# Ending the index stage of an expert-routing step on GpSimd instead of VectorE, in a two-layer decoder kernel on one Trainium2 core

## The reference

```python
    sv, si = lax.top_k(sc, PEER_TOPK)
    cand = sv[:, :, 0, :, None] + sv[:, :, 1, None, :]
    cidx = si[:, :, 0, :, None] * PEER_NKEYS + si[:, :, 1, None, :]
    cs, cpos = lax.top_k(cand.reshape(t, PEER_HEADS, -1), PEER_TOPK)
    idx = jnp.take_along_axis(cidx.reshape(t, PEER_HEADS, -1), cpos, axis=-1)
    gate = jax.nn.softmax(cs, axis=-1)
...
        act = jax.nn.gelu(jnp.einsum('td,tkd->tk', xbb, u_tab[ib], preferred_element_type=jnp.float32))
        return jnp.einsum('tk,tkd->td', gb * act, v_tab[ib].astype(jnp.float32))
```

## Time and profile before

| | |
|---|---|
| median of 3 runs | 1553.53 us (1551.04 to 1553.55) |
| profiled execution, its own time | 1553.37 us |
| its span in the profile | 1551.6 us |
| busy, share of the span | PE 71%, PEld 22%, DVE 72%, ACT 50%, POOL 38% |
| chain that ended last | DMA 32%, DVE 31%, PE 22%, ACT 7% |
| moved by DMA | 603.39 MB, mean 389 GB/s |
| gathers (software queue) | 536.90 MB, 84.8% of the DMA engines' time |

### The profile page before, as it was taken

One profiled execution on the slowest core, in us unless ns is written; L12 is line 12 of the kernel. 1 busy time (PEld: TensorE's weight loads), 2 busy tenths in 40 slices (PEclk: granted clock), 3 DMA queues, 4 the chain that ended last, 5 costly groups with the idle time before them and its releaser, 6 DMA issues.

```text
span 1551.6 us, 19133 instructions
## 1 busy us (share of the span) xinstructions
PE 1097.8 (71%) x5920; PEld 348.4 (22%) x5920; DVE 1111.5 (72%) x2533; ACT 770.2 (50%) x2120; POOL 589.4 (38%) x517
## 2 busy tenths in 40 slices
PE   7997678866765666679866575656878666666665
PEld 3542222322211212223221121212323111111110
DVE  2356887479787899985477799999456866666554
ACT  2315554445456667764334666766334644444433
POOL 0024343323443354554334345344432443434430
PEclk9998689878966776879988567686998777676675
DMA  9569999999999998999999999999999999999995
GB/s 358 179 234 413 420 405 418 414 415 408 415 421 421 354 374 358 410 421 415 412 413 414 403 357 369 355 363 406 380 416 415 415 422 421 421 421 421 421 422 234
DMA packets 105418, 603.39 MB, mean 389 GB/s; under 512 B 9314, under 2 KB 9442, under 8 KB 39780
## 3 DMA queue, kind: packets, MB, share of 16 engines
q0 software_dynamic: 73728, 536.90, 84.8%
q1 hardware_dynamic: 31588, 65.26, 11.3%
HBM read 601.08 MB, written 1.05 MB: 388 GB/s over the span
## 4 chain that ended last, share of the span: by engine, by line
DMA 32%; DVE 31%; PE 22%; ACT 7%; issue 3%; DVEq 3%; ACTq 1%; POOL 1%; SPq 0%; POOLq 0%
DMA rings<-in_uv_tab_dram,idx 24%; DVE rings L1324 11%; PE ps L715 9%; PE ps L920 8%; DMA wst<-in_wq_dram 7%; DVE mem L1231 2%; PE ps L908 2%; DVE dgs L1324 2%; ACT dgs L667 1%; DVE mem L1213 1%; ACT wgt L664 1%; DMA rings<-in_w_in_dram 1%; DVE mem L1242 1%; ACT L661 1%; DVE mem L1240 1%
## 5 line engine op out<-in xcount | busy, mean ns | idle before, releaser
L920 PE MATMUL ps<-rings,dgs 64*64 64x512 f32 x3648 | 638.0, 804 | 343.3 <-ACT dgs L667 342.6
L463 POOL DMA_INDIRECT rings<-in_uv_tab_dram,idx x456 | 521.7, 1144 | 804.3 <-PE ps L920 687.8
L1324 DVE CUSTOM_DVE_ANT_0 rings<-rings,h 128x1024 f32<-128x1024 f32 x456 | 550.7, 1224 | 210.8 <-DMA rings<-in_uv_tab_dram,idx 197.7
L661 ACT ACTIVATE gel<-dots 128x1 f32<-128x1 f32 x512 | 102.1, 199 | 522.2 <-DVE dots L1324 518.5
L920 PEld LDWEIGHTS ps<-rings,dgs 64*64 64x64 f32 x3648 | 128.3, 163 | 783.4 <-ACT dgs L667 682.3
L667 ACT ACTIVATE dgs<-cst,wgt 128x128 f32<-128x128 f32 x512 | 205.6, 402 | 36.3 <-issue 1.5
L715 PE MATMUL ps<-wst,hT 128*128 128x512 f32 x320 | 168.0, 666 | 37.1 <-DMA wst<-in_wq_dram 20.5
L664 ACT ACTIVATE wgt<-gel,share 128x1 f32<-128x1 f32 x512 | 150.8, 295 | 35.5 <-issue 0.3
L920 PE MATMUL ps<-dgs 64*64 64x512 f32 x448 | 80.2, 795 | 53.2 <-ACT dgs L667 53.1
L463 POOL DMA_INDIRECT dgs<-in_uv_tab_dram,idx x56 | 65.9, 1176 | 88.3 <-PE ps L920 74.8
L715 PEld LDWEIGHTS ps<-wst,hT 128*128 128x128 f32 x320 | 63.4, 212 | 138.1 <-issue 134.9
(11 more groups left out here) (192 smaller groups left out, 991.2 us busy)
## 6 DMA issues: line engine op xcount, KB each, us to landing
wst<-in_wq_dram SPq DMA_DIRECT2D x15, 2048.0 KB, 28.2
wst<-in_w_out_dram SPq DMA_DIRECT2D x4, 2048.0 KB, 22.8
wst<-in_glu_w_dram SPq DMA_DIRECT2D x4, 2048.0 KB, 31.7
rings<-in_uv_tab_dram,idx POOLq DMA_INDIRECT x456, 15.7
rings<-in_w_in_dram SPq DMA_DIRECT2D x3, 2048.0 KB, 16.7
rings<-in_w_in_dram SPq DMA_DIRECT2D x2, 1024.0 KB, 7.5
dgs<-in_w_in_dram SPq DMA_DIRECT2D x1, 2048.0 KB, 19.4
vec<-in_vecs_dram SPq DMA_DIRECT2D x3, 512.0 KB, 17.2
```

The source lines that it names most:

```text
L463: nc.gpsimd.indirect_dma_start(out=ring[g % RING], out_offset=None, in_=uv_tab, in_offset=bass.IndirectOffsetOnAxis(ap=idx[n % AHEAD][:, s ...
L661: A.activation(gel[i][:, every], dots[i][:, every], ACT.Gelu_apprx_tanh)
L920: ins = PE.matmul(ps[64 * b:64 * b + 64, 4 + 2 * t + half, :], diag[rows, g % DIAGS, rows], ring[g % RING][rows, D + b * BANK:D + (b + 1) ...
L1324: V.tensor_tensor_reduce(out=u, in0=u, in1=h[:, t, :], scale=1.0, scalar=0.0, op0=ALU.mult, op1=ALU.add, accum_out=dots[n % 2][:, s:s + 1] ...
```

## The change

DVE now does the whole of `route_best` and the first half of the index stage in one go at slot R+4: the four bits and the comparison, into a tile of its own, `hot_p`. The last steps go to POOL: product with the key numbers (512 elements per partition), four additions that each halve the last axis (256, 128, 64 and 32 elements), one addition of the two halves (16) and a copy to the integer tile (16), with a drain behind each. The factor 128 is now put into `top_f` on DVE. POOL runs stages of the table six slots late (`POOL_LAG`): the route whose index stands at R+6 is done right before gather R+12. A new semaphore, `pos_ok`, tells POOL that the one-hot tile is there; DVE waits for the index of the route before (`idx_ok`) before it writes `top_f` anew. Route 0, ahead of the loop, stays on DVE (`route_first`).

```diff
-ROUTE_ALL = [(name, 0) for name, _ in ROUTE]
+ROUTE_ALL = [("route_first" if name == "route_index" else name, 0) for name, _ in ROUTE]
...
+            def route_index(n):
+
+                pool.wait_ge(pos_ok, n)
+                nc.gpsimd.tensor_tensor(hot2, hot2, top_f[:, :, :].unsqueeze(2).to_broadcast([P, 2, TOPK, TOPK]), ALU.mult)
+                pool.drain()
+                for w in (8, 4, 2, 1):
+                    nc.gpsimd.tensor_tensor(hot[:, :, 0:w], hot[:, :, 0:w], hot[:, :, w:2 * w], ALU.add)
+                    pool.drain()
+                nc.gpsimd.tensor_tensor(hot2[:, 0, :, 0], hot2[:, 0, :, 0], hot2[:, 1, :, 0], ALU.add)
+                pool.drain()
+                nc.gpsimd.tensor_copy(idx[n % AHEAD][:, :], hot2[:, 0, :, 0]).then_inc(idx_ok, 1)
...
             for g in range(GROUPS * TOPK):
                 n, s = g // TOPK, g % TOPK
+                if g >= POOL_LAG:
+                    run(WORK[(g - POOL_LAG) // TOPK].get((g - POOL_LAG) % TOPK, []))
...
-            hot = cand[:, :].rearrange("p (a k) -> p a k", k=TOPK)
-            hot2 = cand[:, :].rearrange("p (i a k) -> p i a k", i=2, k=TOPK)
+            hot = hot_p[:, :].rearrange("p (a k) -> p a k", k=TOPK)
+            hot2 = hot_p[:, :].rearrange("p (i a k) -> p i a k", i=2, k=TOPK)
...
-                V.tensor_scalar(top_f[:, 0, :], top_i[:, 0, :], float(NK * (n // (T * PH))), None, ALU.add)
+                if n:
+                    dve.wait_ge(idx_ok, n)
+                V.tensor_scalar(top_f[:, 0, :], top_i[:, 0, :], float(NK * (n // (T * PH))), float(NK), ALU.add, ALU.mult)
...
-
-            def route_index(n):
-
                 V.tensor_scalar(pos_ab[:, 0, :], pos_i[:, :], 4, None, ALU.logical_shift_right)
                 V.tensor_scalar(pos_ab[:, 1, :], pos_i[:, :], 15, None, ALU.bitwise_and)
                 dve.drain()
-                V.tensor_tensor(hot, bc(pos_ab[:, :, :].rearrange("p i a -> p (i a)"), [None, TOPK]),
-                                bc(iota16, [2 * TOPK, None]), ALU.is_equal)
-                dve.drain()
+                ins = V.tensor_tensor(hot, bc(pos_ab[:, :, :].rearrange("p i a -> p (i a)"), [None, TOPK]),
+                                      bc(iota16, [2 * TOPK, None]), ALU.is_equal)
+                if n:
+                    ins.then_inc(pos_ok, 1)
+                dve.drain()
+
+            def route_first(n):
```

More of the change, by code:

```diff
@@ L37 @@
 RING = 9
+POOL_LAG = 6
 AHEAD = 16
@@ L288, in trunk @@
         row = sb("row", [P, 2, TOPK])
+        hot_p = sb("hot_p", [P, 512])
         idx = [sb(f"idx{i}", [P, TOPK], U32) for i in range(AHEAD)]
@@ L322, in trunk @@
         r_ok, rd_ok, sn_done, dt5_ok, dd_ok = (sem(n) for n in ("r_ok", "rd_ok", "sn_done", "dt5_ok", "dd_ok"))
+        pos_ok = sem("pos_ok")
         sq_done, ms_done, sd_done, h_done, nT_done, hT_act, hT_dve, x_done, w_used = (sem(n) for n in (
@@ L453, in _, with run @@
                                     channel_multiplier=-1).then_inc(sgm_ok, 1)
+            hot = hot_p[:, :].rearrange("p (a k) -> p a k", k=TOPK)
[10 more added lines that the diff above has]
+                nc.gpsimd.tensor_copy(idx[n % AHEAD][:, :], hot2[:, 0, :, 0]).then_inc(idx_ok, 1)
+            stage = dict(route_index=route_index)
+            def run(stages):
+                for name, *args in stages:
+                    if name in stage:
+                        stage[name](*args)
             for g in range(GROUPS * TOPK):
                 n, s = g // TOPK, g % TOPK
+                if g >= POOL_LAG:
+                    run(WORK[(g - POOL_LAG) // TOPK].get((g - POOL_LAG) % TOPK, []))
                 if s == 0:
@@ L1307, in route_index @@
                 dve.drain()
-                V.scalar_tensor_tensor(idx[n % AHEAD][:, :], row[:, 0, :], float(NK), row[:, 1, :], ALU.mult,
+                V.scalar_tensor_tensor(idx[n % AHEAD][:, :], row[:, 0, :], 1.0, row[:, 1, :], ALU.mult,
                                        ALU.add).then_inc(idx_ok, 1)
@@ L1331, in _ @@
                          s5_frac=s5_frac, s5_add=s5_add, s5_scan=s5_scan, s5_back=s5_back, glu_sum=glu_sum, norm_r=norm_r)
-            stage |= dict(route_keys=route_keys, route_pairs=route_pairs, route_best=route_best, route_index=route_index,
+            stage |= dict(route_keys=route_keys, route_pairs=route_pairs, route_best=route_best, route_first=route_first,
                           route_gate=route_gate)
```

## The result

The changed kernel takes 1777.28 us (median of 4 runs, 1775.64 to 1779.11) against 1553.54 us of the kernel before beside it. The ratio is 1.1443, 95% interval 1.1423 to 1.1463: 14.4% slower. The forecast was 1560.3 us, 1541 to 1572. The sign was right and the size was wrong by a factor of more than thirty. The span of the profiled execution is 1773.7 us.

What follows compares the result with a forecast made beforehand. DVE was taken to bound the 315 us of S5 stages, DMA nearly all the rest; 7 x (2.6 - 1.62) = 6.9 us on top of 1553.37 us gave 1560.3 us, range 1541 to 1572.

Steps and rivals of the forecast that it cites:

- What bounds the kernel: In the S5 stages, 520 to 660 and 905 to 1080 us, DVE bounds for 315 us; DMA nearly all the rest.
- What is removed: Product, reduction and integer leave DVE: 1.62 us per route, 11.3 us over seven S5 routes; nothing in the other 24.
- what only moves: Two bit operations and the comparison run on DVE at R+4 instead of R+6, same length: costed at nothing.
- POOL's own time: The seven added POOL instructions take 2.6 us per route, bounds 1.65 and 3.9 us.
- Does POOL hold up DVE: Beside POOL's stage, DVE loses the whole of POOL's time, 2.6 us per route; in S5 stretches net 6.9 us lost.
- What the seven instructions delay: Gather R+12 and those behind it in POOL's queue go out later, covered by up to 12 us of queue: cost nothing.
- The third rival: Stage so long that the DMA queue runs empty, by drains and short rows: 1608 us at 14 us; chance 0.10.
- 1200 to 1500 us is unchanged at 420 GB/s: Sign that the forecast is right: the late window keeps its transfer rate.
- a rate below 415 GB/s behind each stage in the late stretch: Sign that the forecast is wrong: the queue ran empty.
- The signs of the hold: In S5 stretches some dots and scans exceed 1.3 us; DVE's busy time falls by far less than 43 us.

Runs made afterwards that it cites:

- the relief alone: Kernel before with product, reduction and integer left out on DVE in routes 1 to 31, a small instruction writing another index: 1544.65 us.
- moved routes: Kernel before, all on DVE, with five routes starting at other slots so that four whole routes leave the S5 stretches: 1541.36 us.
- the semaphore version: Changed kernel with its six POOL drains per route replaced by waits for a semaphore that the instruction before raises: 1564.83 us.
- the seven routes: POOL's index stage, with semaphores, only in routes 13 to 15 and 20 to 23, the others on DVE as in the kernel before: 1561.75 us.
- The extra product: Kernel with POOL's stage in seven routes only, plus one more 512-element POOL product in each of them: 1566.73 us.

## Why the prediction was wrong, step by step

**What bounds the kernel: right in the main.** The S5 stretches are under DVE; the relief alone gave 8.5 us of the 11.3 us, and moved routes gave 11.6 us. Overlooked was 340 to 398 us, where the dots hardly wait for gathers either; slice 10 of the earlier trace rows has DVE at 9 tenths.

**What is removed, what only moves: right in kind.** The 11.3 us lack the 3.0 us that routes 15 and 20 give back as a wait for ACT, and the moved comparison, which I cost at nothing, costs 2.2 us there by the same wait.

**POOL's own time: too low.** The least times of the seven instructions in the semaphore version are 1.26, 0.72, 0.45, 0.29, 0.24, 0.24 and 0.20 us, 3.4 us in sum, where I took 2.6 us; the upper bound of 3.9 us held. With the drains between them it is 4.4 us in the late route above: 1.26 us and then 3.2 us from the first addition to the end of the copy (1514.73 to 1517.90 us).

**Does POOL hold up DVE: yes, but not for the whole of POOL's time.** A dot of 2.29 us beside a product of 1.26 us shows that it does. My sum for it, 6.9 us, stands against 8.3 us in the seven routes and 11.7 us in all, part of which arises outside, where I had put nothing. That 8.3 is near 6.9 is luck. I had DVE lose 2.6 us per route, all of POOL's time; it lost 1.6 us, about half of POOL's 3.4 us, and 5.3 us came from a wait that the sum did not have. The Trainium skill (SBUF — State Buffer, "Who interferes with whom") has the second to come blocked for the whole of the first; the dot's 1.07 us over nearly agrees: it began 0.06 us behind a product of 1.26 us. The extra product, which cost 0.7 us of 1.26, does not refute that, since at times it is POOL that comes second.

**The step that failed is "What the seven instructions delay".** It let the stage take 3.5 to 7.4 us of waiting and 2.6 us of work, all of it covered by 12 us of queue, and passed over the six drains as if they were free. The drain behind the product does not end before the gathers issued ahead of it have landed. It turned a stage of 8 us into a pause in the issuing of gathers of 21 us in the mean (23 us in the late route), and no queue built of nine buffers covers that, since the drain waits for this very queue to empty. The third rival named drains and an empty queue, with 0.10, but as instructions that take long, at 48 us for 2 us beyond the cover. The term left out is 99.9 us for emptying the queue + 112.6 us for what stands behind the drain = 212.5 us, 6.9 us per route.

Of the expected signs, "1200 to 1500 us is unchanged at 420 GB/s" failed, and "a rate below 415 GB/s behind each stage in the late stretch" is what came. The signs of the hold (dots and scans over 1.3 us, DVE's busy time not 43 us less) came too.

## What to carry to other kernels

A drain on POOL, where POOL also issues the gathers, costs the landing of the gathers in flight. Order dependent instructions there by a semaphore that the instruction before raises; if a drain is needed, put it directly ahead of the next gather, since once the queue is empty, nearly all that stands between costs its time. Before moving work from DVE to POOL, ask what DVE reads beside it. Where DVE was the bound with two-input instructions, POOL's reads cost what they saved (11.5 against 11.3 us); taking whole routes out of these stretches was worth 11.6 us, more than the 8.5 us of leaving out the three instructions. And before counting work that leaves an engine, look for another engine's chain that it covers: in two of the seven routes here nearly all the relief became a wait for ACT.

## What the runs showed of the hardware

A POOL drain behind gathers ends only behind the last landing (the first addition came 0.76 us after the start of the dot that had waited for it, and behind the last packet in all 31 routes), and costs 1.4 us even when the last gather has landed; between arithmetic instructions the idle time at it is 0.14 us. A DVE instruction with two SBUF inputs is held up by a POOL instruction that reads SBUF, 1.07 us by a product of 1.26 us; over seven stages of 3.4 us of POOL's own work DVE lost 11.5 us. POOL is held in turn: a copy of 16 elements took up to 1.0 us instead of 0.20, and in the kernel before the 162 gathers issued during a dot took 1.45 us in the mean, where the median of all is 0.94 us. A two-input POOL product of 512 elements takes 1.26 us, an addition of 16 elements 0.24 us.
